# Hyena and attention trunk on one core: the in-projection of layer 0 in two halves of its sum

## What is computed

```python
mod = c_act @ w_ada[i] + b_ada[i]
sh1, sc1, g1, sh2, sc2, g2 = jnp.split(mod, 6, axis=-1)
h = modulate(rms_norm(x, norm1_g[i]), sh1, sc1)
proj = h @ w_in[i]
u_hy, q, k, v, gate_hy, gate_at = jnp.split(proj, split_idx, axis=-1)
y_hy = hyena_mixer(u_hy, ...)
```

## Time and profile before

| | us |
|---|---|
| median of 3 runs | 1072.77 (1072.67 to 1073.19) |
| the profiled execution | 1076.52 |
| its span in the trace | 1074.7 |
| TensorE busy | 1030.8 (96%) |
| VectorE busy | 562.2 (52%) |
| ScalarE busy | 191.2 (18%) |
| loads | 332.83 MB, mean 310 GB/s |

### The profile page before, as it was taken

One profiled execution on the slowest core, in us unless ns is written; L12 is line 12 of the kernel. 1 busy time (PEld: TensorE's weight loads), 2 busy tenths in 40 slices (PEclk: granted clock), 3 DMA queues, 4 the chain that ended last, 5 costly groups with the idle time before them and its releaser, 6 DMA issues.

```text
span 1074.7 us, 18429 instructions
## 1 busy us (share of the span) xinstructions
PE 1030.8 (96%) x7779; PEld 623.0 (58%) x7779; DVE 562.2 (52%) x1186; ACT 191.2 (18%) x396; POOL 20.3 (2%) x40
## 2 busy tenths in 40 slices
PE   7999999999989999999989999999999999999895
PEld 4788667658877344433438875775777634444231
DVE  3377696668776422351324678754558632222123
ACT  4121100311125113101121110031112510111002
POOL 3000000000000000000000000000000000000000
PEclk9999999999999999999999999999999999999898
DMA  9997845269683999999999975535576499999993
GB/s 310 391 387 258 310 159 195 101 215 339 272 362 139 410 385 423 419 421 420 421 401 391 333 254 195 186 119 194 209 297 238 148 422 420 421 420 421 421 420 138
DMA packets 90922, 332.83 MB, mean 310 GB/s; under 512 B 5020, under 2 KB 5355, under 8 KB 66005
## 3 DMA queue, kind: packets, MB, share of 16 engines
q1 hardware_dynamic: 87905, 323.56, 77.1%
q0 software_dynamic: 2048, 6.09, 1.6%
q10 hardware_dynamic: 884, 1.97, 0.6%
HBM read 330.54 MB, written 1.05 MB: 309 GB/s over the span
## 4 chain that ended last, share of the span: by engine, by line
PE 82%; DVE 8%; DMA 5%; issue 2%; SPq 1%; ACT 1%; DVEq 0%
PE bank L763 79%; DMA ring<-in_moe_w_dram 3%; DMA area<-in_moe_w_dram 2%; SPq L693 1%; PE bank L1036 1%; PE bank L1255 1%; DVE wide L1701 0%; DVE area L1892 0%; PE bank L1086 0%; DVE wide L1897 0%; DVE area L1895 0%; DVE area L1893 0%; DVE area L1894 0%; PE bank L816 0%; DVE wide L1896 0%
## 5 line engine op out<-in xcount | busy, mean ns | idle before, releaser
L763 PE MATMUL bank<-ring,hT 128*32 128x512 f32 (+3 forms) x1808 | 283.6, 551 | 5.6 <-DMA ring<-in_moe_w_dram 2.8
L763 PE MATMUL bank<-hT,ring 128*32 128x256 f32 (+1 forms) x2112 | 213.9, 380 | 0.2 <-DVE hT L1735 0.2
L763 PEld LDWEIGHTS bank<-ring,hT 128*32 128x32 f32 (+2 forms) x1808 | 120.1, 134 | 135.7 <-issue 130.5
L763 PEld LDWEIGHTS bank<-hT,ring 128*32 128x32 f32 (+1 forms) x2112 | 159.0, 132 | 54.9 <-issue 8.7
L763 PE MATMUL bank<-ring,area 128*32 128x512 f32 (+1 forms) x744 | 117.9, 566 | 1.5 <-ACT area L1583 0.9
L763 PE MATMUL bank<-area 32*64 32x64 f32 (+5 forms) x648 | 96.1, 363 | 0.0
L2312 DVE TENSOR_TENSOR area<-bank,area 128x512 f32<-128x512 f32 x14 | 9.7, 692 | 131.3 <-PE bank L763 131.3
L763 PE MATMUL bank<-wide,hT 128*32 128x512 f32 (+1 forms) x376 | 76.8, 584 | 0.0
L763 PEld LDWEIGHTS bank<-ring,area 128*32 128x32 f32 (+1 forms) x744 | 43.8, 120 | 54.1 <-issue 49.1
L763 PEld LDWEIGHTS bank<-area 32*64 32x64 f32 (+4 forms) x648 | 43.7, 145 | 51.7 <-issue 50.4
L1701 DVE SCALAR_TENSOR_TENSOR area<-ring,wide,area 128x512 f32<-128x512 f32 x84 | 63.0, 750 | 2.2
(11 more groups left out here) (297 smaller groups left out, 1118.6 us busy)
## 6 DMA issues: line engine op xcount, KB each, us to landing
ring<-in_moe_w_dram SPq DMA_DIRECT2D x136, 1024.0 KB, 15.4
ring<-in_w_in_dram SPq DMA_DIRECT2D x26, 2048.0 KB, 11.4
ring<-in_w_ada_dram SPq DMA_DIRECT2D x24, 2048.0 KB, 13.9
wide<-in_moe_w_dram SPq DMA_DIRECT2D x32, 1024.0 KB, 12.2
cst<-in_moe_w_dram SPq DMA_DIRECT2D x13, 1024.0 KB, 14.6
area<-in_moe_w_dram SPq DMA_DIRECT2D x11, 1024.0 KB, 14.5
ring<-in_w_out_dram SPq DMA_DIRECT2D x4, 2048.0 KB, 7.8
ring<-in_w_br_h_dram SPq DMA_DIRECT2D x4, 1536.0 KB, 6.7
```

Of the source, the lines that this page charges most:

```text
L763: return pe.matmul(dst, lhsT, rhs, start=start, stop=stop, skip_group_check=True)
```

## The change

- EARLY changes the order of w_ada's first four blocks to 0, 2, 1, 3: shift and scale of channels 0 to 511 come first. The third in that order (n = 2) is no longer done by ada(2) and ada_copy(2), but by 8 ada_parts on VectorE; n = 3 stays on TensorE.
- w_in blocks 0 and 1 are loaded as two halves of 1 MiB each, by rows: channels 0 to 511 ("in"), 512 to 1023 ("rest"). The order is w_ada 0, 1, in 0, w_ada 2, in 1, w_ada 3, rest 0, rest 1, w_ada 4, then in 2, w_ada 5 and so on.
- first_shift_and_scale(half), to_h(j) and transposes_to_h(half) do each half by itself. xn of both tiles is made by VectorE. ScalarE does the squares between the sines, and the root before the decays.
- TensorE does the first 4 of 8 products of chunks 0 to 7 (chunks 4 to 7 in the upper half of the banks, u_part), with taps 3 to 7, ada(3), ada_post 2 and 3 and the second transposes among them; then the other 4 of each, with evacuations behind. taps 0 and 1 and the vectors' transposes come before ada(1). Most keep_clock matmuls are gone.
- PARTS_FIRST says how many ada_parts VectorE does after each chunk (32 in all by chunk 17, as before). Both butterflies come before the first evacuation.
- GpSimd waits for "rest" 0 in place of w_in block 0.

The diff, without its context and without renamed counts of semaphores:

```diff
@@ -64,6 +64,9 @@
+EARLY = (0, 2, 1, 3)
+AHEAD = 8
+PARTS_FIRST = (0, 0, 1, 1, 1, 1, 2, 2, 3, 3, 3, 3, 2, 2, 2, 2, 2, 2)
@@ -511,11 +514,18 @@
-            yield from (("ada", b) for b in range(N_EARLY) if L == 0)
-            for b in range(8):
-                yield "in", b
-                if N_EARLY + b < N_LATE:
-                    yield "ada", N_EARLY + b
+            if L == 0:
+                yield from (("ada", 0), ("ada", 1), ("in", 0), ("ada", 2), ("in", 1), ("ada", 3), ("rest", 0), ("rest", 1),
+                            ("ada", N_EARLY))
+                for b in range(2, 8):
+                    yield "in", b
+                    if N_EARLY + b - 1 < N_LATE:
+                        yield "ada", N_EARLY + b - 1
+            else:
+                for b in range(8):
+                    yield "in", b
+                    if N_EARLY + b < N_LATE:
+                        yield "ada", N_EARLY + b
@@ -553,6 +563,12 @@
+                elif kind == "rest":
+                    first = (L, "in", b, None)
+                    space, low = plan[first][:2]
+                    u = low + 1
+                    plan[key] = space, u, landings[u] + 16, []
+                    free = [f for f in free if f[0] // 2 != low // 2] + [(low, first), (u, first)]
@@ -573,7 +589,7 @@
-                return (p_ada, b + 1) if L == 0 and b < N_EARLY else (v_ada, L * N_ADA + b + 1)
+                return (p_ada, (1, 2, 0, 3)[b]) if L == 0 and b in (0, 1, 3) else (v_ada, L * N_ADA + b + 1)
@@ -692,6 +711,15 @@
+                elif L == 0 and (kind == "rest" or (kind == "in" and b * 4 < AHEAD)):
+                    h = int(kind == "rest")
+                    sp.dma_start(dst[:, h * 4 * W:(h + 1) * 4 * W].rearrange("p (k f) -> p k f", f=W),
+                                 t["w_in"][0, h * 4 * P:(h + 1) * 4 * P, b * W:(b + 1) * W]
+                                 .rearrange("(k p) f -> p k f", p=P)).then_inc(landing, 16)
+                elif kind == "ada" and b < N_EARLY:
+                    sp.dma_start(dst[:, :].rearrange("p (k f) -> p k f", f=W),
+                                 t["w_ada"][L, :, EARLY[b] * W:(EARLY[b] + 1) * W].rearrange("(k p) f -> p k f", p=P))\
+                      .then_inc(landing, 16)
@@ -723,7 +751,7 @@
-                    _, landing, value = slot(0, "in", 0)
+                    _, landing, value = slot(0, "rest", 0)
@@ -793,27 +821,29 @@
+                        col = (n if l else EARLY[n]) * 4
...
-                            last = mm(bank[0 if l else 6][:, n * 4 + j:n * 4 + j + 1], part[:, j * P:(j + 1) * P],
+                            last = mm(bank[0 if l else 6][:, col + j:col + j + 1], part[:, j * P:(j + 1) * P],
...
-                        pe.wait_ge(v_ada, n)
+                        pe.wait_ge(v_ada, min(n, 2))
...
-                def transposes_to_h():
+                def transposes_to_h(half=None):
...
-                    pe.wait_ge(a_xn1, L + 1)
-                    for k in range(ND):
+                    if L:
+                        pe.wait_ge(a_xn1, L)
+                    for k in range(ND) if half is None else range(4 * half, 4 * half + 4):
...
-                            last = pe.transpose(bank[4 * L + k // 2][:, (k % 2) * SEQ + tt * P:(k % 2) * SEQ + (tt + 1) * P],
+                            last = pe.transpose(turn_bank(L, k // 2)[:, (k % 2) * SEQ + tt * P:(k % 2) * SEQ + (tt + 1) * P],
@@ -873,48 +903,56 @@
-                    taps(0, 0)
-                    taps(1, 0)
-                    keep_clock_short(3, 7)
-                    ada(1)
-                    taps(2, 0)
-                    taps(3, 0)
...
-                    keep_clock(3, 4)
-                    ada(2)
+                    keep_clock(3, 2)
+                    taps(0, 0)
+                    taps(1, 0)
+                    transposes_to_h(0)
+                    ada(1)
...
-                    transposes_to_h()
-                    ada_post(2)
-                    keep_clock(7, 4)
-                    ada(3)
-                    keep_clock_short(7, 3)
-                    ada_post(3)
-                    keep_clock(7, 2)
-                    keep_clock_short(7, 2)
+                    taps(2, 0)
+                    for c in range(AHEAD):
+                        w = block_of("in", c // 4)
+                        if c == 1:
+                            pe.wait_ge(a_dec, 8)
+                        for k in range(ND // 2):
+                            if c == 0:
+                                pe.wait_ge((v_hT, a_hT)[k // 2], k % 2 + 1 if k else 2)
+                            mm(u_part(0, c), w[:, k, (c % 4) * P:(c % 4 + 1) * P], hT[:, k, :],
+                               k == 0 and c < AHEAD // 2, False)
+                        for u in ((3,), (4, 5), (6, 7))[c] if c < 3 else ():
+                            taps(u, 0)
+                        if c == 5:
+                            ada(3)
+                            pe.wait_ge(v_A1, 1)
+                            ada_post(2)
+                        if c == 6:
+                            ada_post(3)
+                            pe.wait_ge(v_kt, 8)
+                            transposes_to_h(1)
...
-                    w = block_of("in", c // 4)
+                    begun = L == 0 and c < AHEAD
+                    w = block_of("rest" if begun else "in", c // 4)
...
-                    for k in range(ND):
+                    for k in range(ND // 2 if begun else 0, ND):
...
-                            pe.wait_ge((v_hT, a_hT)[k // 2 % 2], turned_on if L or k else 2)
-                        last = mm(bank[c % 4][:, 0:SEQ], w[:, k, (c % 4) * P:(c % 4 + 1) * P], hT[:, k, :],
+                            pe.wait_ge((v_hT, a_hT)[k // 2 % 2], turned_on)
+                        last = mm(u_part(L, c), w[:, k, (c % 4) * P:(c % 4 + 1) * P], hT[:, k, :],
...
-                    for u in taps_after(L, c):
-                        taps(u, L)
@@ -1393,13 +1431,9 @@
-                def squares():
-                    for tt in range(NT):
-                        last = sc.activation(xn[:, tt, :], x[:, tt, :], ACT.Square, scale=D ** -0.5,
-                                             accum_out=ss[:, tt:tt + 1])
-                    last.then_inc(a_chain, 1)
-                    sc.wait_ge(a_chain, L * 4 + 1)
-                    sc.activation(rs[:, :], ss[:, :], ACT.Sqrt, bias=eps[:, :]).then_inc(a_sq, 1)
+                def squares(tt):
+                    return sc.activation(xn[:, tt, :], x[:, tt, :], ACT.Square, scale=D ** -0.5,
+                                         accum_out=ss[:, tt:tt + 1])
@@ -1422,19 +1456,24 @@
+                        if s == 0:
+                            sc.wait_ge(s_x, 16 * NT)
+                            squares(0)
+                        elif s == 1:
+                            squares(1).then_inc(a_chain, 1)
+                    sc.wait_ge(a_chain, 1)
+                    sc.activation(rs[:, :], ss[:, :], ACT.Sqrt, bias=eps[:, :]).then_inc(a_sq, 1)
...
-                    sc.wait_ge(s_x, 16 * NT)
-                    squares()
...
-                sc.wait_ge(v_rs, L + 1)
-                sc.activation(xn[:, 1, :], x[:, 1, :], ACT.Copy, scale=rs[:, 1:2]).then_inc(a_xn1, 1)
-                sc.wait_ge(v_A1, L + 1)
+                    sc.wait_ge(v_rs, L + 1)
+                    sc.activation(xn[:, 1, :], x[:, 1, :], ACT.Copy, scale=rs[:, 1:2]).then_inc(a_xn1, 1)
...
+                    sc.wait_ge(v_A1, 3 if L else (j + 1) // 2)
...
-                        sc.activation(hT[:, k, :], bank[4 * L + j][:, (k % 2) * SEQ:(k % 2 + 1) * SEQ], ACT.Identity,
+                        sc.activation(hT[:, k, :], turn_bank(L, j)[:, (k % 2) * SEQ:(k % 2 + 1) * SEQ], ACT.Identity,
@@ -1442,7 +1481,7 @@
-                    sc.activation(dst, bank[c % 4][:, 0:SEQ], ACT.Identity,
+                    sc.activation(dst, u_part(L, c), ACT.Identity,
@@ -1682,7 +1721,7 @@
-                    dv.wait_ge(p_ada, n + 1)
+                    dv.wait_ge(p_ada, min(n + 1, 3))
@@ -1747,13 +1785,24 @@
+                def first_shift_and_scale(half):
+                    dv.wait_ge(p_mod, 2 * half + 2)
+                    part = slice(4 * half, 4 * half + 4)
+                    both = [a[:, 0:2 * ND].rearrange("p (a k) -> p a k", a=2)[:, :, part]
+                            for a in (modT, bank[6], bT[:, 0, :])]
+                    link(dv.tensor_tensor(both[0], both[1], both[2], ALU.add))
+                    dv.scalar_tensor_tensor(A1[:, part], modT[:, ND + 4 * half:ND + 4 * half + 4], 1.0,
+                                            vTs[0][:, R_N1 + 4 * half:R_N1 + 4 * half + 4],
+                                            ALU.add, ALU.mult).then_inc(v_A1, 1)
+                    dv.wait_ge(v_A1, half + 1)
+
...
-                    dv.wait_ge(v_A1, l + 1)
+                    dv.wait_ge(v_A1, l + 2)
@@ -1794,29 +1843,42 @@
-                    decayed(0, 0)
-                    decayed(1, 0)
```

(47 more changed lines are left out.)

11 lines of the change are left out of this document (5 added, 6 removed).

## The result

| | before | after |
|---|---|---|
| median, us | 1072.98 (1072.67 to 1074.0, 4 executions) | 1066.51 (1064.64 to 1068.78, 4 executions) |
| the profiled execution | 1076.52, span 1074.7 | 1068.78, span 1067.0 |
| mean granted clock of the profiled execution | 0.991 | 0.991 |

The ratio is 0.9929, with a 95% interval of 0.9912 to 0.9945: 0.7% faster, 7.6 us by the ratio and 6.5 by the medians. The forecast was 1064.8.

What follows compares the result with a forecast made beforehand. It took TensorE (82% of the chain) as the bound, its prologue waiting for whole loads. Chunk 0 12.9 us earlier, less some 5 of moved work, gives 8.0: 1072.77 - 8.0 = 1064.8 us, range 1063.2 to 1068.6.

Steps and rivals of the forecast that it cites:

- Loads: Prologue loads at 2.8 us per half block: first half of in-block 0 at 25.8, in-block 2 at 62.8.
- ScalarE: Squares between the sines cost nothing; root before the decays at 20.17, all eight decays by 25.4, no table load added.
- Rival B: ScalarE's table switches cost 1.4 us more each, everything from taps(0) 2.8 later, time 1067.6; chance 0.04.
- Chunk 0: TensorE's first in-projection product starts at 29.95 instead of 42.84, 12.9 us earlier.
- From chunk 0 to chunk 8: This TensorE stretch takes 40.6 us instead of 35.68 with the moved work, so chunk 8 starts at 70.5, 8.0 earlier.
- rival D: Prologue clock falls with most keep_clocks gone; slower once low for over 16 us, 1085 at half the stretch; chance 0.04.
- keep_clock "alone is what really disappears": In TensorE's prologue, some 5 of the 12.9 us return as moved work; only the keep_clock fillers are really removed.
- What must not be late: VectorE's work before chunk 8 is ready in time: slack 3.8 us at ada_post(2), 1.9 where TensorE wants ada_copy(3).
- Rival A: VectorE's queue holds up the second half, TensorE losing 2 to 4 us, time 1066.8 to 1068.8; chance 0.11.
- After chunk 8: Loads there wait for TensorE's progress, so the 8.0 us gain is carried to the end without loss.
- Rival C: The gain isn't carried: later loads or another chain set the time, about 1072.8, no change; chance 0.05.
- The total: Whole kernel 8.0 us faster: profiled execution 1068.5, span 1066.7, median 1064.8; chance of a 6 to 9.5 gain 0.74.

Runs made afterwards that it cites:

- whole: The swapped kernel with in-blocks 0 and 1 loaded whole instead of as split halves; median 1065.86 us, ratio 0.9925 to the kernel before.
- the swapped kernel: Changed kernel with the first half of the transposes of xn moved from ahead of ada(1) to behind ada_post(1); median 1066.32 us, ratio 0.9918 to the kernel before.
- fill_late: Changed kernel plus three short keep_clock matmuls between tap 2 and chunk 0; median 1066.0 us, ratio 0.9916 to the kernel before.
- fill_early: Changed kernel plus three short keep_clock matmuls ahead of tap 0; median 1065.15 us, ratio 0.9917 to the kernel before.
- swap_2: The swapped kernel run again unchanged, for comparison on the same chip and a second trace; median 1065.49 us, ratio 0.9914 to the kernel before.
- dve_more: The swapped kernel plus 18 copies on VectorE between the first butterfly and ada_copy(3); median 1072.39 us, ratio 0.9973 to the kernel before.
- act_back: The swapped kernel with ScalarE's old order again (sines, decays, squares, root); median 1074.87 us, ratio 1.0003 to the kernel before.
- late_8: The swapped kernel plus 16 keep_clock matmuls ahead of chunk 0; median 1073.86 us, ratio 1.0004 to the kernel before.
- the filled ones: Two kernels: the swapped kernel with keep_clock matmuls in two prologue gaps (ratio 0.9906), and that with the out-projection stall filled too (0.991).
- before_bare: Kernel before with the keep_clock matmuls around ada(3) and ada_post(3) taken out; median 1075.32 us, ratio 1.0006 to the kernel before.
- r_after: The changed kernel run again unchanged; median 1067.77 us over 6 executions, ratio 0.9934 to the kernel before.

## Why the prediction was right, and where it wasn't

**Loads: right.** First half of in-block 0 at 25.6 (25.8 forecast), third w_ada block at 31.5 (31.4), in-block 2 at 62.2 (62.8). TensorE waits for none of them. That the halves are needed was not claimed, and whole prices them at 0.7 to 0.9.

**ScalarE: right.** Root at 20.04 (20.17), the first decay begins at 21.36 (21.45). The 1.38 us of drain for each switch of tables, which the Trainium skill gives (ScalarE: Activation LUTs, What ACT_TABLE_LOAD costs), are not in this trace: 18.46 plus 1.28 is 19.74, the root starts at 19.75; 20.07 plus 1.28 is 21.35, the decay starts at 21.36. Rival B is out.

**Chunk 0: right**, at 29.95 to the hundredth, which is partly luck, since the start of the kernel alone differs by more than 1 us between executions (ada(0) starts at 17.63 to 19.30 in the traces).

**From chunk 0 to chunk 8: the sum was right, the clock was left out of it.** 40.6 was forecast, the swapped kernel took 40.65, the changed one 43.93. The step that failed is the one that took the granted clock as 1.00 throughout and gave its fall 0.04, as rival D. It falls ahead of chunk 8 in both traces of the changed kernel, and in those of fill_late, fill_early, swap_2, dve_more and act_back (not in those of swap, whole, late_8 and the filled ones). But I had D's price wrong as well: as a rival it needed 16 us at the low level; it comes as 3.4 to 6.8 (10.2 in act_back).

My argument against it was that a gap of 2.04 us before 10.64 was followed by no slower work. I had looked at ada(0), 8 us later. The work right behind the gap says otherwise. In before:

```profile
5.46 2.93 PE L763 MATMUL bank<-cst 128*128 128x256 f32 x6
...
11.69 3.33 PE L763 MATMUL bank<-cst 128*128 128x256 f32 x8
14.95 0.65 PE L763 MATMUL bank<-wide 64*64 64x257 f32 x4
15.53 1.99 PE L763 MATMUL bank<-cst 128*128 128x256 f32 x8
```

The four instructions at 10.64 took 1.12 us, the same four at 14.95 took 0.65; the six keep_clock instructions at 5.46 took 0.49 us each, those at 15.53 0.25. So TensorE worked at half pace before the gap and behind it, and reached full pace only within those at 11.69. The gap stood in a slow stretch, and says nothing of what a gap does to a fast engine. The profile's granted clock reads 1.00 there all the same, so a mean clock doesn't count this stretch. How long it lasts differs: in fill_early and before_bare work is slow until about 16 (and ada(0) starts at 19.3), in late_8 it is fast from 10.37:

```profile
11.57 3.78 PE L791 MATMUL bank<-cst 128*128 128x256 f32 x8
15.28 1.12 PE L791 MATMUL bank<-wide 64*64 64x257 f32 x4
```

```profile
10.37 0.65 PE L791 MATMUL bank<-wide 64*64 64x257 f32 x4 [2.04 <-issue]
10.95 1.99 PE L791 MATMUL bank<-cst 128*128 128x256 f32 x8
```

The first two lines are fill_early's, the others late_8's.

**keep_clock "alone is what really disappears": half right.** before_bare shows that the fillers cost 1.85 us in the trace and, by its ratio, gave about as much back. That taking them away is part of what made the changed kernel's clock fall is likely, not shown: fill_late, fill_early and swap_2 fell each with one of the prologue's last two gaps filled.

**What must not be late: right.** The cover ahead of ada_post(3) was read as 1.9, plus 1.06 of idle on VectorE in the trace after; dve_more found 3.1. Rival A didn't happen. (Its dearer case, 1068.8, was 0.2 us outside the stated range, which was said to take A in.)

**After chunk 8: carried, as said.** late_8 shows it in the trace, to 0.2 us. Rival C is out.

**The total: right for the profiled execution by two errors that cancel.** It was forecast at 1068.5 and took 1068.78. But 3.3 us were lost to the clock in the prologue, and 3.1 came back at two places whose code the change leaves as it is. I had written that the prediction would be wrong if the shift at chunk 8 differed from that at the end: it does, 4.6 against 7.7. Without such events on either side the change is worth about what was said: an estimate from the two traces, each less its 3.3 us, is 1071.4 against 1063.7, 7.7 us. The two executions with the higher mean clock (0.995 and 0.996) took 1064.64 and 1065.19, the forecast 1064.8; the median of all is 1.7 above that.

## What to carry to other kernels

A prologue that waits for whole operands can begin on the half of a sum for which everything is there; the gain is the time to the first product less the work that moves behind it (12.9 less 5 here), and it is carried to the end if later loads wait for progress. In such a change, look for the small chain that is not a load (here ScalarE's root ahead of the decays): without it the ratio was 1.0003. And where fillers held the clock, put useful work in their place, and price each remaining gap twice: once as a wait, once as a stretch at half speed behind it. Leaving no gap is not known to be enough: swap_2 and dve_more fell near 29 with none after 22.0. And before a gap is taken as proof that the clock holds, compare the work right before and right behind it with the same work at full pace.

## What the runs showed of the hardware that I had not expected

- Falls of the clock are not repeatable. The stall of about 2.07 us near 310 was followed by one in the trace of before and by none in the twelve other traces that have it. The gap of 2.04 us at 8.5 was followed by work at full pace in four traces; the clock fell within 1.6 us in three of them (fill_late, swap_2, dve_more) and not in the fourth (late_8). A fall came with no gap over 0.71 us in the 10 us ahead of it (swap_2, low from about 28.6 to 32.0). Before that fall stood products of 32 columns, column sums and transposes; whether these are what counts was not tried.
- The three traces with a fall near 12 all fell again near 29. The five others of the swapped order of work (swap, whole, late_8 and the filled ones; act_back with its long wait aside) had neither. The changed order (r_after and the result's trace, fill_early) fell at 30.4 to 31.0 without one near 12. So what TensorE did far ahead of a place may go with what happens there; this is a pattern in a few traces, and no run tested it.
- A delay of TensorE's work in the prologue cost about twice its length: 4.5 became 9.4 (act_back), 2.8 about 6 (dve_more).
- The start of the kernel differs by up to 1.7 us between executions of the same work (ada(0) at 17.63 to 19.30), before any of the change is reached. The two latest, 19.29 and 19.30, are those in which TensorE worked at half pace until about 16, the earliest the one that was at full pace from 10.37 on.
